# The recurrence's output normalised inside its last pair, and the output projection begun over six of eight channel tiles

## The reference, cut to what matters

```python
mean = jnp.mean(y, axis=-1, keepdims=True)
var = jnp.mean(jnp.square(y - mean), axis=-1, keepdims=True)
y = ((y - mean) * lax.rsqrt(var + LNX_EPS)).reshape(B, S, D)
y = y * lnx_w + lnx_b
y = y + bonus.reshape(B, S, D)
return (y * g).astype(h.dtype) @ w_o
...
x = x + rwkv7_time_mix(h, ...)
h = rms_norm(x, g_ffn[layer])
x = x + swiglu_ffn(h, w_gu, w_down)
```

## Time and profile before

| | |
|---|---|
| median of 3 runs | 1403.82 us |
| lowest, highest | 1401.42, 1408.97 us |
| the profiled execution | 1402.62 us |
| its span | 1400.4 us |
| mean granted TensorE clock | 0.95 of full |
| PE busy in the span | 1255.3 us (90%) |
| DVE, ACT busy | 940.1 us (67%), 630.4 us (45%) |

### The profile page before, as it was taken

The page is one execution under the profiler, slowest core; times in us unless marked ns, Lnnn a source line. Parts: engine busy times, 40 slices in busy tenths (PEclk is TensorE's granted clock), DMA queues, the critical chain, the costliest instruction groups (busy, mean ns, idle before and its releaser), DMA issues.

```text
span 1400.4 us, 21886 instructions
## 1 busy us (share of the span) xinstructions
PE 1255.3 (90%) x9218; PEld 1167.3 (83%) x9218; DVE 940.1 (67%) x1298; ACT 630.4 (45%) x829; POOL 208.5 (15%) x139
## 2 busy tenths in 40 slices
PE   3998989887899999699888889999789887999995
PEld 3887878775899999696667888999789877999995
DVE  6767657544468874755864567774548835999994
ACT  4464343224443445456556564434442244544442
POOL 0000000000264442000000122210000001344431
PEclk9999999898999999899998999999899997999998
DMA  7440001000577764253322668785342213545530
GB/s 269 151 154 31 32 1 61 1 1 1 196 268 246 247 214 154 90 184 117 119 92 95 216 246 286 268 288 181 121 151 91 90 61 120 175 164 185 186 135 30
DMA packets 122656, 200.20 MB, mean 143 GB/s; under 512 B 3264, under 2 KB 111168, under 8 KB 112320
## 3 DMA queue, kind: packets, MB, share of 16 engines
q1 hardware_dynamic: 117664, 168.05, 35.7%
q0 software_dynamic: 3456, 25.17, 4.8%
q10 hardware_dynamic: 1440, 5.60, 1.1%
HBM read 197.75 MB, written 1.05 MB: 142 GB/s over the span
## 4 chain that ended last, share of the span: by engine, by line
PE 63%; DVE 24%; ACT 7%; issue 5%; DMA 0%; DVEq 0%; POOL 0%; ACTq 0%
PE bank L631 13%; PE bank L632 12%; PE bank L633 12%; DVE buf L2390 7%; DVE ring_r L1696 6%; PE bank L714 3%; PE bank L716 3%; PE bank L715 3%; ACT high L1173 2%; DVE work L1952 2%; PE bank L647 2%; PE bank L869 2%; DVE work L1948 2%; PE bank L857 2%; PE bank L1065 1%
## 5 line engine op out<-in xcount | busy, mean ns | idle before, releaser
L631 PE MATMUL bank<-part,high 128*128 128x256 f32 x1664 | 485.8, 292 | 66.6 <-DVE part L1703 61.5
L632 PE MATMUL bank<-part,high 128*128 128x256 f32 x1664 | 481.7, 289 | 0.0
L1696 DVE TENSOR_TENSOR ring_r<-ring,high 128x2048 fp32r<-128x2048 f32 (+1 forms) x155 | 342.9, 2221 | 206.3 <-ACT high L1173 204.0
L633 PE MATMUL bank<-part,ring_r 128*128 128x256 f32 x1664 | 481.1, 289 | 0.0
L631 PEld LDWEIGHTS bank<-part,high 128*128 128x128 f32 x1664 | 329.4, 198 | 75.3 <-issue 52.6
L632 PEld LDWEIGHTS bank<-part,high 128*128 128x128 f32 x1664 | 329.5, 198 | 0.3 <-issue 0.2
L633 PEld LDWEIGHTS bank<-part,ring_r 128*128 128x128 f32 x1664 | 329.1, 198 | 0.0
L1173 ACT ACTIVATE high<-ring 128x2048 fp32r<-128x2048 f32 x155 | 295.2, 1906 | 51.1 <-PE bank L633 40.9
L1623 POOL TENSOR_TENSOR ring_r<-ring,high 128x512 fp32r<-128x512 f32 x44 | 95.4, 2167 | 534.0 <-ACT high L1173 533.9
L714 PE MATMUL bank<-part,high 128*128 128x256 f32 x528 | 151.3, 287 | 9.2 <-POOL part L1617 4.9
L715 PE MATMUL bank<-part,high 128*128 128x256 f32 x528 | 150.1, 284 | 0.0
(11 more groups left out here) (260 smaller groups left out, 1580.9 us busy)
## 6 DMA issues: line engine op xcount, KB each, us to landing
ring<-in_wide SPq DMA_DIRECT2D x122, 1024.0 KB, 5.9
ring<-in_down SPq DMA_DIRECT2D x33, 1024.0 KB, 5.0
buf<-in_wide POOLq DMA_DIRECT2D x24, 1024.0 KB, 7.2
con<-in_cons SPq DMA_DIRECT2D x1, 1472.0 KB, 10.9
ring<-in_wide SPq DMA_DIRECT2D x2, 576.0 KB, 7.0
buf<-in_wide ACTq DMA_DIRECT2D x1, 1024.0 KB, 5.4
buf<-in_wide SPq DMA_DIRECT2D x1, 1024.0 KB, 5.3
buf<-in_ctx_t ACTq DMA_DIRECT2D x1, 1024.0 KB, 4.7
```

The source lines that it names most:

```text
L631: mm(bank, ah, bh, start=start, stop=False, skip_group_check=shared)
L632: mm(bank, ah, bl, start=False, stop=False, skip_group_check=shared)
L633: return mm(bank, al, bh, start=False, stop=stop, skip_group_check=shared)
L1696: v.tensor_tensor(low, raw, hi.bitcast(F32), ALU.subtract).then_inc(sem("unit_low"), 1)
```

## The change

The mean is no longer a sum and a subtraction: one product with a new constant matrix, the identity less 1/64 in each head's block (`centre`), gives y less its mean. ACT squares that from PSUM and copies it back over y (`y_square`).

For pieces 0 to 2 this happens inside the last pair, in the places where earlier pairs prepare the next: the centring products (`y_centre`) stand on PE ahead of level 1, ACT's squares and copies and a table load ahead of its copies of level 1, the variance products (`y_variance`) on PE behind level 1, the logarithms on ACT in levels 1 to 3, the roots in levels 4 to 6. DVE scales and gates piece 0 behind level 6 (`y_out`), pieces 1 and 2 behind the state's update, with the gate's copies and the low parts between. ACT makes the high parts of pieces 0 and 1 behind the copies of sa0 and sa1.

Piece 3 follows the last pair. PE centres it, then begins the output projection: tile 0 over channel tiles 0 to 5, the variance product of piece 3, tiles 1 and 2 over channel tiles 0 to 5, then the last two channel tiles of tiles 0, 1 and 2, and then the whole of tile 3. The banks of this stage are set by hand. The high part of y and the squares use other buffers.

In the diff, a line that is only dots stands for what is left out; eight blanks of indent are cut.

```diff
 
-CONS = [("ident", P), ("ones", P), ("head_sum", P), ("right_left", LEV * P), ("left_right", LEV * P), ("score_mask", 4 * P), ("rope_swap", P), ("cos", S), ("sin", S)]
+CONS = [("ident", P), ("ones", P), ("head_sum", P), ("right_left", LEV * P), ("left_right", LEV * P), ("score_mask", 4 * P), ("centre", P), ("rope_swap", P), ("cos", S), ("sin", S)]
...
         plan_r(p + 1, SIDE_BANKS)
+    else:
+        for j in range(p):
+            place(("yc", j), SIDE_BANKS)
...
             place(("kksum", p + 1), SIDE_BANKS)
+        elif l == 1:
+            for j in range(p):
+                place(("yvar", j), SIDE_BANKS)
...
             place(("l2g", 2 * (p - 2) + (what == "q1")), SIDE_BANKS)
-for n in ("ymean", "yvar"):
-    for j in range(4):
-        place((n, j))
-plan_proj("o")
+place_at(("yc", 3), 4)
+place_at(("yvar", 3), 5)
+for i in range(4):
+    place_at(("o", i), (6, 7, 0, 1)[i])
+    unit_job("o", i // 2, i % 2, ("o", i))
...
            "ao": 9, "ffn1": 0, "hx": 0, "mix": 3, "ffn2": 0}
-HIGH_BUF = {"mix0": 10, "mix4": 8, "mix5": 11, "y": 10, "ffn0": 1, "hc": 10, "hkv": 1, "hq": 3,
+HIGH_BUF = {"mix0": 10, "mix4": 8, "mix5": 11, "y": 4, "ffn0": 1, "hc": 10, "hkv": 1, "hq": 3,
...
           buf[11][:, :, :].rearrange("p (j a) b -> p j (a b)", j=4)]
-y_sq = buf[11]
+y_sq = buf[1]
...
 
+        def y_centre(j):
+            for g in (2 * j, 2 * j + 1):
+                wait_freed(pe, ("yt", g))
+            bank = open_bank(("yc", j))
+            close(mm(bank[:, :], const("centre"), piece(y_t, j), start=True, stop=True), ("yc", j))
+
+        def y_variance(j):
+            pe.wait_ge(sem("y_sq"), j + 1)
+            bank = open_bank(("yvar", j))
+            close(mm(bank[:, :], const("head_sum"), piece(y_sq, j), start=True, stop=True), ("yvar", j))
+
+        def o_tiles(i, kts):
+            w = arrived("o", i // 2, i % 2)
+            bank = bank_of(("o", i)) if kts[0] else open_bank(("o", i))
+            for kt in kts:
+                wait_part("y", kt)
+                for half in range(2):
+                    last = split_mm(bank[:, half * S:(half + 1) * S], [z[:, kt, half * P:(half + 1) * P] for z in w], tile_of("y", kt),
+                                    kt + half == 0, kt == KT - 1, shared=True)
+            if kts[-1] == KT - 1:
+                close(last, ("o", i))
+
...
                 project_r(p + 1)
+            else:
+                for j in range(p):
+                    y_centre(j)
...
                     key_sum(p + 1)
+                elif l == 1:
+                    for j in range(p):
+                        y_variance(j)
...
                     gate_lora(2 * (p - 2) + (what == "q1"))
-        for g in range(NG):
-            wait_freed(pe, ("yt", g))
-        sums_over("ymean", const("head_sum"), y_t, lambda j: None)
-        sums_over("yvar", const("head_sum"), y_sq, lambda j: pe.wait_ge(sem("y_sq"), j + 1))
-        project("o", "y")
+        y_centre(3)
+        o_tiles(0, range(0, 6))
+        y_variance(3)
+        for i in (1, 2):
+            o_tiles(i, range(0, 6))
+        for i in range(3):
+            o_tiles(i, range(6, KT))
+        o_tiles(3, range(0, KT))
...
 
+        def y_square(j):
+            key = ("yc", j)
+            wait_full(eng, key)
+            act_(piece(y_sq, j), bank_of(key)[:, :], ACT.Square).then_inc(sem("y_sq"), 1)
+            release(act_(piece(y_t, j), bank_of(key)[:, :], ACT.Copy), key)
+
+        def y_log(j):
+            key = ("yvar", j)
+            wait_full(eng, key)
+            release(act_(piece(y_sq, j), bank_of(key)[:, :], ACT.Ln, scale=1.0 / CH, bias=eps_lnx), key)
+
+        def y_root(j):
+            wait_freed(eng, ("yvar", j))
+            act_(piece(y_sq, j), piece(y_sq, j), ACT.Exp, scale=-0.5).then_inc(sem("y_root"), 1)
+
...
                 key_square(p + 1)
+            else:
+                for j in range(p):
+                    y_square(j)
+                log_table()
...
                         decay_sums(p + 1)
+                elif l <= 3:
+                    y_log(l - 1)
+                else:
+                    y_root(l - 4)
...
                         units(g)
+                if not nxt and what in ("sa0", "sa1"):
+                    part_of("y", what == "sa1")
...
                 side_out("bkt", p + 1, bk_tok)
-        for j in range(4):
-            eng.wait_ge(sem("y_centered"), j + 1)
-            act_(piece(y_sq, j), piece(y_t, j), ACT.Square).then_inc(sem("y_sq"), 1)
-        rsqrt_of([(("yvar", j), piece(y_sq, j)) for j in range(4)], CH, eps_lnx, "y_root")
-        parts("y")
+        log_table()
+        y_square(3)
+        part_of("y", 2)
+        y_log(3)
+        y_root(3)
+        part_of("y", 3)
...
 
+        def y_out(j):
+            eng.wait_ge(sem("y_root"), j + 1)
+            wait_freed(eng, ("vt", j))
+            two = (2 * j, 2 * j + 1)
+            for kt in two:
+                own.go(v.scalar_tensor_tensor(y_t[:, kt, :], y_t[:, kt, :], pcol("lnx_w", kt), y_sq[:, kt, :], ALU.mult, ALU.mult))
+            own.settle()
+            for kt in two:
+                own.go(v.scalar_tensor_tensor(y_t[:, kt, :], y_t[:, kt, :], pcol("lnx_b", kt), a_t[:, kt, :], ALU.add, ALU.add))
+            own.settle()
+            wait_freed(eng, ("l2g", j))
+            v.tensor_tensor(piece(y_t, j), piece(y_t, j), piece(g_t, j), ALU.mult).then_inc(sem("part_raw"), 1)
+
...
                         tilde_rest(p + 1)
+            if not nxt:
+                y_out(0)
...
                 bonus_out(p + 1)
-            if p >= 2:
-                for j in (2 * p - 4, 2 * p - 3):
-                    gate_out(j)
-
-        for p in range(len(PAIRS)):
-            wait_freed(eng, ("vt", p))
-        own.settle()
-        for g in range(NG):
-            wait_freed(eng, ("yt", g))
-        for j in range(4):
-            key = ("ymean", j)
-            wait_full(eng, key)
-            v.scalar_tensor_tensor(piece(y_t, j), bank_of(key)[:, :], -1.0 / CH, piece(y_t, j), ALU.mult, ALU.add)\
-                .then_inc(sem("y_centered"), 1)
-        eng.wait_ge(sem("y_centered"), 4)
-        for j in range(4):
-            eng.sem_inc(free[jobs[("ymean", j)][0]], 1)
-        for j in range(4):
-            eng.wait_ge(sem("y_root"), j + 1)
-            two = (2 * j, 2 * j + 1)
-            for kt in two:
-                own.go(v.scalar_tensor_tensor(y_t[:, kt, :], y_t[:, kt, :], pcol("lnx_w", kt), y_sq[:, kt, :], ALU.mult, ALU.mult))
-            own.settle()
-            for kt in two:
-                own.go(v.scalar_tensor_tensor(y_t[:, kt, :], y_t[:, kt, :], pcol("lnx_b", kt), a_t[:, kt, :], ALU.add, ALU.add))
-            own.settle()
-            v.tensor_tensor(piece(y_t, j), piece(y_t, j), piece(g_t, j), ALU.mult).then_inc(sem("part_raw"), 1)
-            if j:
-                low_piece("y", j - 1)
+            if p == 2:
+                gate_out(0)
+                gate_out(1)
+            elif p == 3:
+                low_piece("y", 0)
+                y_out(1)
+                gate_out(2)
+                y_out(2)
+                low_piece("y", 1)
+                gate_out(3)
+                low_piece("y", 2)
+
+        y_out(3)
...
     z["head_sum"] = i // CH == j // CH
+    z["centre"] = np.where(i == j, 1.0, 0.0) - np.where(i // CH == j // CH, 1.0 / CH, 0.0)
...
     ci, cj = i % CH, j % CH

```

## The result

The changed kernel took 1396.48 us in the median of 11 executions (1390.37 to 1402.15) against 1403.82 for the kernel before; the ratio is 0.994 with a 95% interval of 0.9914 to 0.9966. That lies in the stated range of 1387.5 to 1400.5, at 7.3 us less between medians where I had said 10.2. But the range covers two rivals as well: the median lies 0.2 us outside the forecast's own part of it (1391.3 to 1396.3) and inside the first rival's (the clock falls in the pair, 1396.3 to 1400). The profiled execution took 1391.34 us with a span of 1389.3: 11.1 us less than the span of before.

What follows compares the result with a forecast made beforehand. One serial path of 46.65 us, from the last output copy to the next norm's logarithm, was taken as the bound. Saving 12.2 less 2.0 gave 10.2 us off 1402.62, 1392.4, stated as 1393.5 for the median; range 1387.5 to 1400.5.

Steps and rivals of the forecast that it cites:

- the forecast's own part: Whole kernel: saving 7.5 to 12.5 us, so 1391.3 to 1396.3 us; chance 0.64.
- the first rival: Last pair's second half: the clock falls there, saving 3.8, up to 7.5 us, time 1396.3 to 1400; chance 0.19.
- What moves out: Last output copy to next norm's logarithm: three pieces' normalisation moves into the pair, 46.65 us becomes 34.4, saving 12.2.
- E: End of the last copy of the recurrence's output, from which the prediction counts times behind the pair.
- the new wait before tile 3: Output projection: PE waits 3.0 us for the fourth weight unit, whose split follows an earlier tile's closing.
- What the pair pays: Last pair: added centrings, variances, squares, copies and roots lengthen its chain by 2.0 us, bounds 1.0 and 7.
- the 0.3 of level 1: Last pair, level 1: ACT's squares, copies and table load delay DVE's join from 283.61 to 283.95, costing 0.3 us.
- The table load: ACT's table load: 1.30 us by the trace; the skill's 2.66 us would make the saving near 7.5 us.
- The sum: Whole kernel: 12.2 less 2.0 gives 10.2 us saved, 1392.4 from the profiled execution, stated as 1393.5.
- PE alone: Projection to norm: splits hidden, PE alone sets the end, no wait before tile 3; saving 16, time 1387.8; chance 0.06.
- A loss: Level 1 to the pair's end: waits and bunched products keep PE at the lower clock, 22 us, 1415; chance 0.05.
- the saving given back: Feed-forward: its units or a transfer hold it up, time within a few us of 1403; chance 0.06.

Runs made afterwards that it cites:

- high halves first: Changed kernel with ACT making the three weight units' high halves before its squares, DVE's order unchanged; 1392.99 us, 0.9906 of the kernel before.
- tile by tile: Changed kernel with the projection's four tiles one after the other over all eight channel tiles, piece 3's variance product first; 1396.91 us, 0.994 of the kernel before.
- two tiles: Changed kernel with two projection tiles, not three, begun over six of eight channel tiles, tiles 2 and 3 whole; 1393.35 us, 0.9927 of the kernel before.
- all three: Changed kernel with two tiles begun early, ACT's high halves first and the variance products spread over three levels; 1386.66 us, 0.9883 of the kernel before.
- spread variances: Changed kernel with one variance product behind each of levels 1, 2 and 3 instead of three behind level 1; 1392.59 us, 0.9919 of the kernel before.
- filled from level 3 on: Changed kernel with overwritten 256-column products in the last pair, ahead of levels 3 to 6's first y products and the last dx products; 1395.32 us, 0.9935.
- the last experiment: Kernel before with three overwritten 512-column products in PE's idle stretch ahead of level 1 of the last pair; 1402.32 us, 0.9993.

## Why the prediction came out as it did

*What moves out.* Right, and close. Tile 0's add stands at E + 16.5 (said 16.7), the new wait before tile 3 is 2.70 us (3.0), the last add at E + 31.6 (32.1), the logarithm at E + 34.13 (34.4). That the splits and not PE's matmuls set the end is shown from two sides: high halves first saves 3.8 us with PE's order unchanged, and PE's order tile by tile, which does without the early start, loses nothing.

*What the pair pays.* The mechanism was right, the size 1.12 us instead of 2.0. ACT's copies and squares follow each other every 0.48 us, not 0.60 (they start at 277.41, 277.91, 278.38), so level 1 lost nothing; the second join comes 1.23 us later, of which 0.23 is the later start of the pair and 1.00 the variances (1.8 forecast, with the 0.3 of level 1). From there to E another 0.12 is lost (0.2 forecast). Spreading them gives 1.24 back.

*The table load.* One load stands at 280.47 for 1.28 us and ACT's next copy at 281.77: 1.30 in all, in the middle of a pair as behind it. The sum was rightly made with the trace's figure.

```profile
277.41 0.60 ACT L1370 ACTIVATE buf<-bank 128x512 f32<-128x512 f32 x1 [5.34 <-PE bank L817]
277.91 0.59 ACT L1371 ACTIVATE buf<-bank 128x512 f32<-128x512 f32 x1
278.38 0.60 ACT L1370 ACTIVATE buf<-bank 128x512 f32<-128x512 f32 x1
...
280.47 1.28 ACT L1191 ACT_TABLE_LOAD   x1
281.77 1.08 ACT L1410 ACTIVATE work<-bank 128x512 f32<-128x512 f32 x2
```

*The sum.* 10.2 us forecast, 11.2 in the profiled execution (369.42 to 358.25), of which 11.1 reach the end of the span.

*The step that failed* is the first rival and its chance of 0.19, with the sentence "Against it: PE gets more work there, not less." I took the clock's drop for an accident beside the forecast. It is the usual case: 16 of 23 executions lie more than 4 us above the fastest, all of them with a mean clock of 0.949 or less, against 0.952 or more for the other seven. Both profiles of the changed kernel are of fast executions, so where its slow ones lose the clock is inferred from its relatives: in the profiles of four kernels with the same or nearly the same pair (tile by tile, high halves first, two tiles, all three) the clock was at its lower level for 10 to 24 us from about 308 to 312 us on, where the three profiles of kernels without work in the pair had none. The profiles of the changed kernel itself (twice) and of the spread variances had no such drop, and 1391 to 1392 us. Over the executions the clock takes 4.3 us of the gain: 12.0 between the fastest, 7.7 between the means. So the median came out inside the range because the mechanism forecast for the saving and the rival came together; that the rival's range began where the forecast's ended hides this. PE did get more work in that pair, but not in its thin levels: filled from level 3 on, six executions show no drop.

What stays open is why the change makes the drop more frequent. The thin stretch is the same code on PE before and after. That PE is no longer idle ahead of level 1 isn't enough, by the last experiment. The bunch of variance products behind level 1 isn't needed for it either: the six executions with spread variances stayed within 5.6 us, but the three edits together spread them too, and there two of six executions, the profiled one among them, had the drop. Whether the place at which the stretch comes matters wasn't tested.

*The other rivals.* PE alone (1387.8) did not come, by the wait ahead of tile 3. A loss did not come, nor was the saving given back later: from the logarithm to the end of the span it is 1030.98 us before and 1031.05 after.

## What to carry to other kernels

When work is moved so that an engine can finish several results at once, look at what is released by each result one after the other: here the residual's adds, squares and weight splits were nearly hidden as long as tiles closed 5.7 us apart, and became the bound when three closed together. Work for a gap should be placed one piece for each gap; three products in one gap cost 1.24 us, one in each of three nothing. And ahead of moving anything, read the granted clock in the stretch: a chain in which PE is thin for a few microseconds may pay for it in the dense work behind. A few products that nobody needs can then be cheaper than the gap: in all four pairs they brought 10 to 11 us, in the last pair alone 1.6 in the median, with the fastest execution 4.5 slower.

## What the runs showed of the hardware

The granted clock does not fall only after PE has been idle. It fell to 1.2 GHz behind levels 5 and 6, in which PE had products of 64 and 128 columns with gaps of 0.1 to 0.7 us between their groups, and stayed there for 10 to 24 us although PE then worked without a gap (24.89 us of 25 in the window from 308 to 333 us of the two tiles' kernel). With products of 256 columns in the gaps it was 1.00 in all three windows at the ends of the earlier pairs, where it had been 0.83, 0.77 and 0.73. In the same profile it was down to 0.50 from 270 to 272, behind the 2.56 us ahead of level 1 of the last pair, which were left empty. That a fall depends on the execution fits what the Trainium skill says (TensorE: Matmul & The Clock Gate, What's actually happening), that the same kernel shows different counts of slow matmuls from run to run, though the page speaks of a kernel's start; that it lasts so long under dense work is not what its "activity releases the throttle" led me to expect.

ACT's copies and squares of 512 columns from PSUM, 0.60 us each in their rows, start 0.47 to 0.50 us apart when nothing holds them.

The trace and the Trainium skill (ScalarE: Activation LUTs, What ACT_TABLE_LOAD costs) differ on the switch of tables: 1.30 us here, wherever it stood, against about 2.66 us there.
